# Pairs of weight quarters beside chunked attention: one sum, one split and one value copy earlier, one decay product later

## The reference, cut to what matters

```python
# one decoder layer, SEQ = D_MODEL = 1024, float32
h = modulate(rms_norm(x), shift1, scale1)
proj = h @ w_in                    # GLA and HGRN2 heads and their gates
# every HGRN2 head, head width 128, chunks of 64 tokens:
forget = lb + (1.0 - lb) * sigmoid(hf)
q, k, v, log_a = silu(hq), 1.0 - forget, hi, log(forget)
cum = cumsum(log_a within a chunk)
q_rel, k_rel = q * exp(cum - cum_mid), k * exp(cum_mid - cum)
k_to_end = k * exp(cum_last - cum)
o = tril(q_rel @ k_rel.T) @ v + (q * exp(cum)) @ state
o = rms_norm(o, hgrn_norm_g) * silu(h_gate)
x = x + gate1 * (concat(o_gla, o_hgrn) @ w_out)
x = x + gate2 * (square(relu(h2 @ w_mlp1)) @ w_mlp2)
return rms_norm(x, final_norm_g)
```

## Time and profile before

| | |
|---|---|
| median of 3 runs | 1164.46 us (1162.1 to 1164.61) |
| the profiled execution, its own time | 1164.09 us |
| its span from first to last instruction | 1162.3 us |
| busy in the span: TensorE, VectorE, ScalarE, GpSimd | 1133.2, 865.7, 613.0, 496.9 us |
| mean granted TensorE clock | 0.993 |
| the three heads and the gates | from about 225 to 436 us of the span |

### The profile page before, as it was taken

The page is one execution under the profiler, slowest core; times in us unless marked ns, Lnnn a source line. Parts: engine busy times, 40 slices in busy tenths (PEclk is TensorE's granted clock), DMA queues, the critical chain, the costliest instruction groups (busy, mean ns, idle before and its releaser), DMA issues.

```text
span 1162.3 us, 15518 instructions
## 1 busy us (share of the span) xinstructions
PE 1133.2 (97%) x5483; PEld 935.7 (81%) x5483; DVE 865.7 (74%) x1033; ACT 613.0 (53%) x933; POOL 496.9 (43%) x320
## 2 busy tenths in 40 slices
PE   7999999999999999999999999999999999999996
PEld 6788788777878788888888888888888888888885
DVE  6898887778677767377976765677795875966876
ACT  7763555757566566255654555455663533524424
POOL 1021122144343345427525353344466675666741
PEclk9999999989999999999999999999999999999998
DMA  9778387344353536721455344544624637437203
GB/s 359 260 235 271 129 210 203 77 127 123 101 168 106 151 104 227 239 90 75 140 167 182 136 155 135 181 143 160 190 63 161 227 91 262 162 128 275 69 2 145
DMA packets 162948, 186.71 MB, mean 161 GB/s; under 512 B 7604, under 2 KB 119352, under 8 KB 159928
## 3 DMA queue, kind: packets, MB, share of 16 engines
q1 hardware_dynamic: 160472, 179.44, 46.6%
q0 software_dynamic: 2400, 6.29, 2.8%
HBM read 138.51 MB, written 40.89 MB: 154 GB/s over the span
## 4 chain that ended last, share of the span: by engine, by line
PE 89%; DVE 3%; DMA 3%; ACT 2%; issue 1%; SPq 1%; POOL 0%; DVEq 0%; ACTq 0%
PE unit_bank L1782 19%; PE unit_bank L2220 9%; PE unit_bank L2221 9%; PE unit_bank L2222 9%; PE small_bank L2220 9%; PE small_bank L2221 9%; PE small_bank L2222 9%; PE small_bank L1782 4%; PE unit_bank L2067 3%; PE unit_bank L2069 3%; PE unit_bank L2068 3%; DMA ada_slot<-in_w_ada_dram 1%; PE small_bank L1821 1%; PE small_bank L1924 1%; DVE ada_acc L2321 1%
## 5 line engine op out<-in xcount | busy, mean ns | idle before, releaser
L1026 POOL TENSOR_TENSOR wr_lo<-quarter,wr_hi 128x512 fp32r<-128x512 f32 x122 | 198.1, 1635 | 174.2 <-ACT wr_hi L1570 174.1
L2220 PE MATMUL unit_bank<-op_hi,wr_hi 128*128 128x512 f32 x452 | 176.8, 391 | 0.2 <-issue 0.2
L2222 PE MATMUL unit_bank<-op_hi,wr_lo 128*128 128x512 f32 x452 | 176.2, 390 | 0.0
L2221 PE MATMUL unit_bank<-op_lo,wr_hi 128*128 128x512 f32 x452 | 176.1, 390 | 0.0
L2220 PE MATMUL small_bank<-op_hi,wr_hi 128*128 128x512 f32 x448 | 174.7, 390 | 0.0
L2221 PE MATMUL small_bank<-op_lo,wr_hi 128*128 128x512 f32 x448 | 174.5, 389 | 0.0
L2222 PE MATMUL small_bank<-op_hi,wr_lo 128*128 128x512 f32 x448 | 174.5, 389 | 0.0
L1570 ACT ACTIVATE wr_hi<-wr_full 128x512 fp32r<-128x512 f32 x90 | 56.8, 631 | 173.3 <-DVE wr_full L2986 165.6
L1570 ACT ACTIVATE wr_hi<-quarter 128x512 fp32r<-128x512 f32 x136 | 83.0, 626 | 90.2 <-PE unit_bank L2222 51.2
L2986 DVE TENSOR_TENSOR wr_full<-quarter,quarter 128x512 f32<-128x512 f32 x90 | 89.2, 992 | 55.4 <-PE small_bank L2222 23.7
L1782 PE MATMUL unit_bank<-a_hi,w_hi 128*128 128x512 f32 x304 | 121.2, 399 | 0.0
(11 more groups left out here) (382 smaller groups left out, 2368.0 us busy)
## 6 DMA issues: line engine op xcount, KB each, us to landing
quarter<-in_w_mlp_dram SPq DMA_DIRECT2D x128, 256.0 KB, 4.1
hidden_scratch<-hid SPq DMA_DIRECT2D x98, 256.0 KB, 2.3
ada_slot<-in_w_ada_dram SPq DMA_DIRECT2D x48, 512.0 KB, 6.7
op_full<-hidden_scratch SPq DMA_DIRECT2D x21, 1024.0 KB, 4.8
pair_quarter<-in_w_in_dram SPq DMA_DIRECT2D x32, 256.0 KB, 4.0
piece_x<-t_scratch SPq DMA_DIRECT2D x16, 512.0 KB, 4.1
piece_y<-t_scratch SPq DMA_DIRECT2D x32, 256.0 KB, 3.5
raw<-in_w_out_dram SPq DMA_DIRECT2D x16, 512.0 KB, 4.5
```

Source lines behind the costliest of these rows:

```text
L1026: pool.tensor_tensor(wr_lo[slot][:, :, :], split_source(n), wr_hi[slot][:, :, :].bitcast(F32), ALU.subtract).then_inc(wr_lo_pool, 1)
L2220: pe.matmul(dst, wh, ah, start=opens, stop=False, skip_group_check=True)
L2221: pe.matmul(dst, wh, al, start=False, stop=False, skip_group_check=True)
L2222: mm = pe.matmul(dst, wl, ah, start=False, stop=k == KH - 1, skip_group_check=True)
```

## The change

What it does, engine by engine:

- **ScalarE.** `output`: the squares are rounded to `sq_hi` straight from the PSUM bank (a Square written in the rounded type), ahead of the square into `stat` and the copy, and no longer from `stat`; the number of instructions is the same. In the late pair `norm_log(1)` and `norm_exp(1)` go behind the roundings for P7 and P2 and the second value copy.
- **VectorE, late pair.** S4 goes from behind the `q_rel` product to right behind join "11". `low_squares(1)` goes ahead of the `cum` product. `far_keys` goes behind join "21", `norms(1)` behind join "12", and `far_queries` leaves the late pair for the next pair, behind its S1 (`gates` takes it over for the last head).
- **VectorE.** `low_squares` waits for `stat` as well. In `gates`, `low_squares(0)` goes ahead of S2.

```diff
                     src = bank_of("o", half)
                     act.wait_ge(normed, before("o", gi) + half)
+                    act.activation(sq_hi[:, 0, :], src, ACT.Square).then_inc(sq_hi_ready, 1)
                     act.activation(stat[:, 0, :], src, ACT.Square).then_inc(o_squared, 1)
                     act.activation(tok(mixed[:, gi + 1], half), src, ACT.Copy).then_inc(read["o"], 1)
-                    act.wait_ge(o_squared, before("o", gi) + half + 1)
-                    act.activation(sq_hi[:, 0, :], stat[:, 0, :], ACT.Copy).then_inc(sq_hi_ready, 1)
...
                 value_of(1, late, "22")
-                norm_log(1)
-                norm_exp(1)
                 pair_high(late + 1, P7)
                 pair_high(late + 1, P2)
                 value_of(0, late, "21")
+                norm_log(1)
+                norm_exp(1)
                 tanh_of(t0, 1, late, "12")
...
                     dve.wait_ge(sq_hi_ready, before("split", gi) + half + 1)
+                    dve.wait_ge(o_squared, before("o", gi) + half + 1)
...
                 weight_sum_of(early, "S1")
+                if early:
+                    far_queries(cum_of(gi - 1), gi - 1)
...
                 join(late, "11")
+                weight_sum_of(late, "S4")
...
+                low_squares(1)
...
-                low_squares(1)
...
-                weight_sum_of(late, "S4")
...
                 weight_sum_of(late + 1, "S3")
-                far_keys(gi)
                 weight_sum_of(late + 1, "S2")
                 join(late, "21")
-                far_queries(own_cum, gi)
+                far_keys(gi)
+                join(late, "12")
                 norms(1)
-                join(late, "12")
                 silu_of(t0, 1, late, "12", made + 4)
...
+                low_squares(0)
                 weight_sum_of(late, "S2")
-                low_squares(0)
```

## The result

The changed kernel takes 1176.74 us (median of 4 runs, 1176.35 to 1179.06) against 1163.31 us of the kernel before (4 runs, 1162.1 to 1164.61): a ratio of 1.0123, 95% interval 1.0107 to 1.0138 (the two medians are 1.0115 apart). That is 13 to 14 us slower. The forecast was 10.1 us slower; its direction and its chain of causes held, its size was short by a quarter of what was measured. The profiled execution has a span of 1175.1 us at a mean clock of 0.987. One execution of this document stands apart, 2646.18 us in e2 at a granted clock of 1.00, with no trace of it; the ratios leave it out.

A forecast was written before the change was run, and what follows sets the result against it. TensorE bounds the kernel (busy 1133.2 of 1162.3 us), held at boundaries by value copies and by tanh and SiLU of "12". Three boundaries at 1.07 + 2.5 give +10.7, gates -0.6: +10.1, so 1174.5 us; 8-in-10 range 1166.0 to 1177.5.

The forecast's parts named there:

- the contention: Late pair: GpSimd's subtraction for P3 gets between two VectorE products and costs 1.1 us, bounds 0 to 1.3.
- the falling clock: TensorE at each boundary: idle of 4.6 us in one piece drops the clock, costing 2.5 us, bounds 0 to 3.3.
- the gain in the gates: Gates: low_squares(0) ahead of S2 cuts TensorE's wait for sq_lo from 1.0 to 0.4 us, gaining 0.6.
- the chain's term: Each of three boundaries: SiLU of "12" starts at 287.1 instead of 286.04, delaying the seventh product's piece, +1.07 us.
- The second chain: Boundary: the seventh product's piece waits for tanh and SiLU of "12"; tanh comes 4.44 us behind the second value copy.
- the 4 to 5 that were to show it: Sign in the new profile: the seventh product's piece waits 4 to 5 us for VectorE's t, three times.
- GpSimd between `cum` and `q_rel`: Late pair, VectorE: the subtraction for P3 gets in between these two products; 1.1 us lost, q_rel done at 276.9.
- The early `sq_lo`: Early pair, VectorE: started sooner, sq_lo is still held to the same moment by GpSimd; value 0, bounds 0 to 0.5 us.
- the landing of quarter 0: Late pair: next quarters land up to 3 us sooner, ending ScalarE's 1.91 us wait; P1's rounding starts at 277.4.
- The clock holds: Rival, boundaries: same chain without slow stretches, +2.6 us, 1167.1, or 1169.6 with one fall; chance 0.20.
- GpSimd costs nothing: Rival, late pair: VectorE keeps its place between cum and q_rel, but the clock falls; +6.9 us, 1171.4; chance 0.12.
- The waits are really gone: Rival: SiLU of "12" ready by 283.3, each boundary gains 3.5 us; -11, 1153.4; chance 0.07.

The follow-up runs named there:

- e2: Changed kernel with ScalarE's norm_log(1) and norm_exp(1) back in their old place, ahead of the rounding for P7: 1162.32 us, ratio to before 0.9989.
- e6: Kernel before with only the squares rounded from the bank and the low squares ahead of S2 in the gates: 1161.75 us, a single run.
- e9: Changed kernel with quarter 0 of the next pair issued ahead of the 512 KB piece in SyncE's queue: 1167.48 us, ratio to before 1.004.
- e1: Changed kernel with 14 useless matmuls between value transposes and the seventh product's first piece at each boundary: 1167.72 us, ratio to before 1.0032.
- e3: Changed kernel with S4 back behind the q_rel product: 1175.36 us, ratio to before 1.0093.
- e8: e7 with S4 back behind the q_rel product as well: 1159.55 us, ratio to before 0.9973.
- e7: e4 with the second half's norm, its product and gate moved on into the next pair: 1160.74 us, ratio to before 0.9981.
- e10: e7 with quarter 0 issued ahead of the 512 KB piece in SyncE's queue: 1158.56 us, ratio to before 0.9963.
- e4: Changed kernel with the tanh of "12" ahead of the norm on ScalarE, and join "12", far_keys, SiLU ahead of norms(1) on VectorE: 1166.99 us, ratio 1.004.
- e5: Changed kernel with 5 useless matmuls between value transposes and the seventh product's first piece at each boundary: 1169.2 us, ratio to before 1.0053.

## Why the prediction was right in kind and short in size

In short: the chain, the contention, the falling clock and the gain in the gates were right in kind. The step that failed is the size of the chain's term: +1.07 us a boundary was put down, 1.76, 1.97 and 1.86 were measured, because quarter 0 came to be used hardly sooner and GpSimd's next subtraction then held S3. The clock's term was short too, 2.5 put down and 2.87 to 2.91 measured. The rise between the medians, 13.4 us, lies just beyond the 13.0 between the 1164.5 that the forecast started from and its upper bound of 1177.5; that 1176.74 is still below 1177.5 is luck, since the kernel before came out at 1163.31 here.

*The second chain.* Right. The piece waited for the SiLU of "12" and not for the value copies; the tanh came 4.44 us behind the second copy (281.89 to 286.33), just the length taken from the earlier trace rows, and the norm product in front cost what was put down. e2 shows that this one move carries the loss. The gap was 3.67 us, less than the 4 to 5 that were to show it.

The Trainium skill (ScalarE: Activation LUTs, What ACT_TABLE_LOAD costs) puts a switch of tables at 2.66 us, more than half of it a drain. The trace after does not agree: the load takes 1.28 us, and the whole row of copy, load, Ln, load and Exp fits into 4.44 us, which leaves no room for two such drains.

*GpSimd between `cum` and `q_rel`.* Right: 2.12 us, 0.9 extra where 1.1 was put down. The early `sq_lo`, costed at nothing for the same reason, cost and gave nothing (e6).

*The step that failed: the landing of quarter 0, and with it "S3 starts at 279.85" and S2 0.7 later.* It rested on the quarters landing "up to 3 us sooner, so that ScalarE no longer waits". S4 did come sooner, but the quarters 0 and 1 were then issued right behind 768 KB of other transfers and not into an emptier queue. SyncE's queue, in the kernel before:

```profile
272.67 0.50 SPq L728 DMA_DIRECT2D piece_x<-t_scratch  x1
275.82 0.93 SPq L745 DMA_DIRECT2D pair_quarter<-in_w_in_dram  x2
```

and in the changed one:

```profile
272.00 0.51 SPq L728 DMA_DIRECT2D piece_x<-t_scratch  x1
272.60 0.93 SPq L745 DMA_DIRECT2D pair_quarter<-in_w_in_dram  x2
```

The head started 0.7 us earlier in this run than in that of before (256.44 against 257.12), so 0.7 has to be added to its times to compare them with the forecast's. So counted, the quarters were issued at 273.3, 2.5 us sooner than before, but quarter 0 was used at 278.4, only 0.5 us sooner (0.15 and 0.3 at the other two boundaries); the forecast has 277.4. ScalarE still waited 0.98 us for it. GpSimd's subtraction for P1 began at 279.1 and not 278.1, and so it lay on S3, which it held for 1.1 us, and not on the end of the gate product for 0.3. S3 began sooner than forecast, at 279.4, but took 1.78 us, and S2 came at 281.2 and not 280.55; all behind it, to the piece at 288.6 in place of 287.9, is as late. e9 takes just this away and has A at 1.0 to 1.2 us over before, where the forecast had +1.07. So this term was 0.8 us a boundary too small, 2.4 in all.

*The clock.* Right in kind, mis-sized by 0.4: B grew by 2.87, 2.87 and (without the gain in the gates) 2.91 us, 2.5 was put down; 1.15 in all. e1 confirms it: its three B are 8.6 us shorter together, of 9.0 between the medians. Two things here were luck. That all three falls cost the most was not certain: e3, with nearly the same gap, had 1.3, 1.6 and 2.9. And the row that the forecast argued from, the fall ahead of the first paired head, is no sure one: all twelve profiled executions of this document have the same idles of 1.0 and 1.5 us there, and only five a fall (before, the change, e3, e6, e8).

*A wait that the forecast did not have.* P3 waits for join "22", and the late `q_rel` made it late: 1.18 us at each boundary. It costs nothing at the end, since the piece ends later anyway, but splits the gap: 3.67 us of idle in one piece and not 4.6.

*Gates.* Right: the wait fell from 1.01 to 0.41 us (to 0.41 in e6 as well).

*The sum* with the measured terms: 1.76 + 1.97 + 1.86 + 2.87 + 2.87 + 2.91 - 0.6 = 13.6 us, against 13.4 between the medians. That they agree so well is in part chance: the spans of the two profiled executions differ by 12.8. The 0.8 between lies outside the heads' A and B: from the value transposes to the first early pair's sum of squares the changed kernel took 1.7 us less (31.81 against 33.50; the clock fell there in both, for longer in the kernel before), ahead of that 1.0 us more, and behind the gates 0.2 less.

*The rivals.* "The clock holds" is what e1 made: 1167.7, where 1167.1 was given; but over the kernel before beside it, that is +4.7 where +2.6 was given, since the chain's term is too small there as well. "GpSimd costs nothing" is not what e3 made: with `q_rel` free of it, S3 and S2 waited, and A stayed 1.4 to 1.8 us over before. "The waits are really gone" needs the norm out of the chain, and even then (e7) other waits of 1.2 us take the place, 0.45 in e10.

## What to carry to other kernels

Before a wait is shortened, look at what the waiting engine waits for next: here the second chain ended 0.1 us before its use and was in no list of waits. Work that fills an engine's idle time is free only there; moved between two links of a chain it adds its whole length there: the tanh stood 0.5 us behind the second value copy and then 4.44. And idle time of TensorE has a form as well as a sum: at the boundaries pieces of up to 1.4 us cost only themselves, one piece of 3.7 cost 2.9 more, so that adding useless matmuls made the changed kernel 9 us faster.

## What the runs showed of the hardware that was not expected

- The clock's reaction is not settled by the length of the gap alone: in these profiled runs 2.4 to 2.5 us of idle led to a fall at one boundary of three, 2.9 us at one of three, 3.5 and 3.7 at all of them, at 1.3 to 2.9 us of lost time each. Two idles of 1.0 and 1.5 us with 8 small matmuls between them, ahead of the first paired head, led to one in five executions of twelve.
- An earlier release can be worth little: issued 2.5 us sooner within the head, but right behind two others, quarter 0 took 5.1 us from its issue to its use in place of 3.1, and was used 0.15 to 0.5 us sooner. With quarter 0 issued ahead of the 512 KB piece (e9) ScalarE did not wait for it.
- The fall ahead of the first paired head costs less than its slow stretch. From the value transposes to the first early pair's sum of squares it took 31.8 to 33.5 us with a fall and 31.5 to 31.8 without one, for in these (e1, e2, e4, e5, e7) TensorE waited 1.36 to 1.60 us for `sq_lo` in place of 0.18 to 0.19. Only with quarter 0 issued first (e9, e10) there was neither, and it took 30.9 and 30.5.
